# The last third of each layer's modulation on VectorE as products summed along rows, in place of TensorE

## The reference, cut to what matters

```
mod = (jax.nn.silu(cond) @ lw['w_ada'] + lw['b_ada'])[:, None, :]
shift1, scale1, gate1, shift2, scale2, gate2 = jnp.split(mod, 6, axis=-1)
h = rmsnorm(x, lw['norm_mix']) * (1 + scale1) + shift1
mix, new_ctx = token_mixers(h, lw, lam_init, ropes, ctx)
x = x + gate1 * (mix @ lw['w_out'])
h = rmsnorm(x, lw['norm_ffn']) * (1 + scale2) + shift2
x = x + gate2 * moe_ffn(h, lw)
```

## Time and profile before

| what | value |
|---|---|
| median of 3 runs | 1346.04 us (1345.32 to 1348.03) |
| the profiled execution's own time | 1347.21 us |
| its span, first to last instruction | 1345.4 us |
| TensorE busy | 1232.7 us (92%), mean granted clock 0.971 |
| VectorE busy | 273.3 us (20%) |
| ScalarE busy | 235.9 us (18%) |
| read from HBM | 493.60 MB |
| the chain that ended last | PE 69%, DMA 24%, DVE 2% |

### The profile page before, as it was taken

How to read it: one execution, slowest core, us unless ns; L and a number is a source line. 1 busy time by engine, 2 the same in 40 slices (tenths; PEclk the granted TensorE clock), 3 DMA queues, 4 the chain that set the end, 5 groups by cost and what they waited for, 6 DMA issues and landing times.

```text
span 1345.4 us, 22750 instructions
## 1 busy us (share of the span) xinstructions
PE 1232.7 (92%) x9612; PEld 841.1 (63%) x9612; DVE 273.3 (20%) x714; ACT 235.9 (18%) x521; POOL 2.8 (0%) x13
## 2 busy tenths in 40 slices
PE   6999999999998889888999999999999889888986
PEld 4566687667765565556565668866667565546554
DVE  1252342110011010101034424411011010101012
ACT  2363131110010101000134431311010101010102
POOL 0000000000000000000000000000000000000000
PEclk8999999999998899899999999999999999889999
DMA  9889849999999999999956663999999999999992
GB/s 385 323 318 343 349 190 403 372 422 420 421 420 422 422 422 422 422 421 422 410 203 260 246 242 151 416 373 420 421 418 420 422 422 420 420 422 423 421 420 93
DMA packets 80657, 496.58 MB, mean 369 GB/s; under 512 B 10576, under 2 KB 12880, under 8 KB 24784
## 3 DMA queue, kind: packets, MB, share of 16 engines
q1 hardware_dynamic: 76528, 493.63, 89.6%
q10 hardware_dynamic: 4064, 2.00, 0.5%
HBM read 493.60 MB, written 2.00 MB: 368 GB/s over the span
## 4 chain that ended last, share of the span: by engine, by line
PE 69%; DMA 24%; DVE 2%; issue 1%; SPq 1%; ACT 1%; DVEq 0%; ACTq 0%
DMA dn<-in_exp_w_down 20%; PE PS L2146 15%; PE PS L2180 13%; PE PS L2078 8%; PE PS L2085 7%; PE PS L1650 7%; PE PS L1982 4%; DMA gu<-in_exp_w_gate 3%; PE PS L1574 2%; PE PS L2044 2%; PE PS L1606 2%; DMA gu<-in_w_in 1%; PE PS L1773 1%; PE PS L1784 1%; PE PS L2122 1%
## 5 line engine op out<-in xcount | busy, mean ns | idle before, releaser
L2146 PE MATMUL PS<-gu,arena 128*32 128x256 f32 (+1 forms) x3072 | 318.5, 382 | 1.8 <-issue 1.8
L2146 PEld LDWEIGHTS PS<-gu,arena 128*32 128x32 f32 (+1 forms) x3072 | 186.6, 118 | 78.1 <-issue 19.7
L2180 PE MATMUL PS<-arena 128*64 128x512 f32 (+1 forms) x336 | 172.6, 662 | 61.4 <-DMA dn<-in_exp_w_down 59.8
L2180 PE MATMUL PS<-dn,arena 128*32 128x512 f32 (+1 forms) x688 | 180.4, 628 | 0.0
L2078 PE MATMUL PS<-arena 128*128 128x128 f32 x1408 | 176.3, 278 | 0.5 <-ACT arena L1024 0.5
L2078 PEld LDWEIGHTS PS<-arena 128*128 128x128 f32 x1408 | 164.1, 192 | 17.9 <-issue 16.7
L2085 PE MATMUL PS<-arena 128*128 128x256 f32 x704 | 160.2, 380 | 1.4 <-ACT arena L1006 1.4
L2146 PE MATMUL PS<-arena 128*64 128x256 f32 (+1 forms) x672 | 152.0, 379 | 0.0
L2085 PEld LDWEIGHTS PS<-arena 128*128 128x128 f32 x704 | 130.2, 190 | 20.5 <-ACT arena L1006 3.2
L1485 DVE TENSOR_TENSOR arena<-arena,PS 128x256 f32<-128x256 f32 x44 | 18.5, 421 | 563.4 <-ACT arena L1020 563.4
L1006 ACT ACTIVATE arena<-PS 128x512 f32<-128x512 f32 x88 | 52.5, 597 | 453.1 <-PE PS L2180 453.1
(11 more groups left out here) (257 smaller groups left out, 1022.9 us busy)
## 6 DMA issues: line engine op xcount, KB each, us to landing
gu<-in_exp_w_gate SPq DMA_DIRECT2D x106, 1024.0 KB, 16.0
gu<-in_exp_w_up SPq DMA_DIRECT2D x86, 1024.0 KB, 17.6
dn<-in_exp_w_down SPq DMA_DIRECT2D x86, 1024.0 KB, 17.6
arena<-in_exp_w_up SPq DMA_DIRECT2D x42, 1024.0 KB, 15.1
arena<-in_exp_w_down SPq DMA_DIRECT2D x42, 1024.0 KB, 17.1
gu<-in_w_ada SPq DMA_DIRECT2D x20, 2048.0 KB, 9.0
xh<-in_exp_w_gate SPq DMA_DIRECT2D x22, 1024.0 KB, 11.4
gu<-in_w_in SPq DMA_DIRECT2D x8, 2048.0 KB, 13.5
```

Of the source, the lines that this page charges most:

```text
L2146: ins = mmul(PS[w * h:w * h + w, 5, FF * half:FF * half + FF], xg[:, k, w * h:w * h + w], weights[half][:, k], start=(k == 0), stop=(k == ...
L2180: ins = mmul(PS[w * h:w * h + w, 7 - n, :], hidT[:, j * P + w * h:j * P + w * h + w], weights[:, j, 512 * n:512 * n + 512], start=(j == 0) ...
```

## The change

The third of the modulation that holds scale2 and gate2 leaves TensorE in both layers. The host turns its part of w_ada so that each partition holds, for one output element, the whole row of 1024 weights, and gives the conditioning as one row too. On the core, both conditioning vectors are broadcast over all partitions (1 MB, in a new tile cond_rows in the arena), ScalarE forms their Silu in place, and VectorE forms each output as a product of two 128x1024 operands that is summed along its row (accum_out): 8 chunks x 2 vectors x 2 groups, 32 instructions a layer. The weights come as four pieces "rows" of 2 MB through the same ring, in place of four modulation pieces. The products themselves go to a scratch tile. ROW_STEPS spreads the 32 steps over eleven places of VectorE's queue; the pieces 0 to 3 are freed by steps 8, 16, 24 and 32, the last of which stands behind the fourth update of x. ADA_AT has 8 pieces for layer 0 (from the third at P3) and 4 for layer 1, one of them in the norm; LOADED_EARLY is longer.

```
-ADA_AT = [{"P3": [4, 5], "P4": [6], "UQ": [7], "M": [8, 9], "P0a": [10], "P0b": [11], "P1a": [12, 13], "P1b": [14, 15]},
-          {"P3": [17], "P4": [18], "UQ": [19], "M": [20], "P0a": [21], "P0b": [22], "P1b": [23]}]
-ADA_NORM = {2: 16}
-ADA_BY = [4, 6]
+ADA_AT = [{"P3": [4, 5], "P4": [6], "UQ": [7], "P0a": [8, 9], "P0b": [10], "P1a": [11]},
+          {"P3": [13], "P4": [14], "UQ": [15]}]
+ADA_NORM = {2: 12}
+ADA_BY = [3, 4]
+ROW_STEPS = {"even3": 8, "even4": 4, "result4": 2, "masked": 5, "result5": 2, "mixed": 2, "keys": 2, "turned": 3,
+             "step1": 2, "step2": 1, "step3": 1}
 LOADED_EARLY = [(("w_in", 0, 2), ("chunks", 0, 2)), (("w_in", 0, 3), ("chunks", 0, 2)), (("mla", 0, 0), ("ada", 0, 6)),
-                (("w_in", 0, 0), ("ada", 0, 10)), (("w_in", 0, 1), ("ada", 1, 0))]
+                (("w_in", 0, 0), ("ada", 1, 0)), (("rows", 0, 0), ("ada", 1, 1)), (("w_in", 0, 1), ("ada", 1, 3)),
+                (("rows", 0, 1), ("ada", 1, 3)), (("w_out", 0, 1), ("rows", 0, 2)), (("w_out", 0, 0), ("rows", 0, 3)),
+                (("w_out", 1, 1), ("rows", 1, 2)), (("w_out", 1, 0), ("rows", 1, 3))]
...
-        out.append(("w_in", l, 0))
+        out += [("w_in", l, 0), ("rows", l, 0)]
         ada(l, "P0b", "P1a")
         out.append(("w_in", l, 1))
         ada(l, "P1b")
+        out += [("rows", l, q) for q in range(1, ROW_PIECES)]
         out += [("w_out", l, 1), ("w_out", l, 0)]
...
+                    if it == (("ada", 0, 4), ("mla", 1, 0))[l]:
+                        if l > 0:
+
+                            sp.wait_ge(S["down_done"], ROUNDS * l)
+                        sp.dma_start(cond_rows.rearrange("p g k -> p (g k)"), t["cond_rows"].partition_broadcast(P)
+                                     ).then_inc(S["cond_in"], 16)
...
                 for j in range(RING - 1):
-                    sp.wait_ge(S["weights_used"], ends[l] - RING + j + 1)
+                    wait_used(sp, last_in[l][j])
                     load_fixed(j, l)
...
                 exps(4)
+                act.wait_ge(S["cond_in"], 16 * (l + 1))
+                A(cond_rows, cond_rows, ACT.Silu).then_inc(S["cond_spread"], 1)
+
+                A(small[:, 501:502], col("eps"), ACT.Exp)
...
+            def ada_rows(l, at):
+
+                for _ in range(ROW_STEPS[at]):
...
+                    if i == 0:
+                        v.wait_ge(S["cond_spread"], l + 1)
+                    if j + g == 0:
+                        v.wait_ge(gu_loaded[item_slot[it]], loaded_at[it])
+                    ins = stt(products, gu[:, item_slot[it], j * D:j * D + D], 1.0, cond_rows[:, g], ALU.mult, ALU.mult,
+                              accum_out=mod[:, l, 4 + what, c, g:g + 1])
+                    if (j, g) == (ROW_CHUNKS - 1, G - 1):
+                        ins.then_inc(S["rows_used"], 1)
+                        v.wait_ge(S["rows_used"], ROWS_TOLD * l + 3 * what + q % 2 + 1)
+                        if c == NC_ - 1:
+                            tt(mod[:, l, 4 + what], mod[:, l, 4 + what], bc(b_ada[:, l, 4 + what], 2, G), ALU.add
+                               ).then_inc(S["rows_used"], 1)
+                    else:
+                        link(ins)
...
                 ada_lag(l, "P0a")
+                ada_rows(l, "even3")
                 latent_results(3)
                 even_half(4)
                 ada_lag(l, "P0b")
+                ada_rows(l, "even4")
                 negated_max(5)
...
                 ada_lag(l, "P1a")
+                ada_rows(l, "result4")
                 even_half(5)
...
                     if b > 0:
                         add_squares(STEPS[0][b - 1])
+                    if 0 < b < 4:
+                        ada_rows(l, f"step{b}")
```

## The result

The changed kernel takes 1371.24 us (median; 1369.84 to 1372.59) where the kernel before takes 1346.89 (1345.32 to 1348.03) in the same series: ratio 1.0174, 95% interval 1.016 to 1.0188, slower. That is +24.4 us; the forecast was +6.8. The profiled executions differ by 22.6 us (spans 1368.0 and 1345.4).

What follows compares the result with a forecast made beforehand. TensorE's chain was taken to bound each layer's first stage, weight bytes at 422 GB/s the expert stage. Layer 0: 0.7 + 5.0 - 4.5 = +1.2; layer 1: 3.1 + 5.0 - 2.5 = +5.6; 1346.04 + 6.8 = 1352.8 us, range 1337 to 1360.

Steps and rivals of the forecast that it cites:

- The product, 1.33 us: VectorE's 128x1024 product with row sum: 1.33 us a step, bounds 1.26 and 1.43, 42.6 us a layer.
- Rival C: Products with sum on VectorE run at half rate, each step 1.07 us more: 1400 us; chance 0.06.
- The stage up to the output projection: Before the expert stage: layer 0's gain shrinks from 8.4 to 0.6 us; layer 1's is lost, +0.5, +1.1 for the broadcast.
- Rows piece 1: Layer 0: this 2 MB weight piece lands at about 127.6 us and VectorE waits for it, 4 to 5 us.
- the maximum of unit 5: VectorE, layer 0: starts at 132.9 us, behind 4 steps, where it started at 127.40; +5.5.
- the broadcast: SyncE's 1 MB conditioning rows ahead of layer 1's latent weights: +1.1 us, bounded by 0 and 2.5; nothing in layer 0.
- The release, +0.7 and +3.1: Start of the expert weight stream: 186.7 us against 186.05 in layer 0, +3.1 us against 835.56 in layer 1.
- The one product that I had counted behind the updates: One VectorE step (1.33 + 0.03 us) behind the fourth update of x, counted in the release.
- The expert out of the hole, +5.0 less the gaps: Fixed expert 0's 2 MB load leaves the stream's hole: +5.0 us a layer, less 4.5 (layer 0) and 2.5 (layer 1).
- the gaps: Holes in the expert stream's first 60 us that a later stream fills: 4.5 us in layer 0, 2.5 in layer 1.
- VectorE against TensorE: First stage: VectorE's steps hold TensorE and eat the 8.4 us a layer taken from it.
- rival A: VectorE's steps fit its idle spans and don't hold TensorE, each layer keeps 8.4 us: 1334.6 us, faster; chance 0.22.

Runs made afterwards that it cites:

- e1: Changed kernel with VectorE's wait for the layer's six output stores moved from ahead of the first update of x to behind the last; 1362.96 us.
- e2: Changed kernel with SyncE waiting for the layer's six stores before it issues the shared weights, VectorE's wait left in place; 1361.92 us.
- e5: Kernel before, shared weights held until the retention output is turned, fixed expert 0 until the output weights are used, no new VectorE work; 1350.05 us.
- e14: Changed kernel with the edits of e1 and e12 together; 1359.46 us, +12.0 against the kernel before.
- e4: Kernel before with one wait changed: fixed expert 0 loaded only when the output weights are used up; 1349.15 us, +2.65.
- e6: Changed kernel with 36 matmuls of 2 columns with 128-column weights added at TensorE's start; 1383.71 us.
- e12: Changed kernel with 36 matmuls of 2 columns with 2-column weights added ahead of the first norm's sums in each layer; 1369.05 us.
- e7: Changed kernel with each product over 8 of its 1024 columns, loads, order and waits kept, third modulation vectors not the reference's; 1350.31 us.
- e10: Changed kernel with e1's edit, w_out piece 0 loaded ahead of rows piece 2, and products 17 to 32 behind the mix; 1363.94 us.
- e11: e10 with each product over 8 of 1024 columns, third modulation vectors not the reference's; 1338.02 us.

## Why the prediction was wrong

The direction was right, the size outside the range. Point by point:

**The product, 1.33 us: right enough.** 1224 ns, 1.27 from one to the next, near the lower end of my bounds. The read of the accumulator is recorded as 0.08 us and lies under the product's end. Rival C is dead, and by the same row so is the rule of the Trainium skill (Vector Engine (DVE) Microarchitecture Reference, section "Points that are easy to get wrong") for this case: by it the product would take twice as long and the kernel 1400 us; the trace doesn't agree, the form with a sum costs what the plain product costs.

**The stage up to the output projection: right in layer 1, 2.6 us short in layer 0.** Rows piece 1 was waited for until 127.12 (127.6 forecast), the maximum of unit 5 started at 132.20 (132.9); with the early start allowed for, both are about 1 us later than forecast. In layer 1, from its start, it was 93.6 where it was 92.7 before, and the output projection 116.9 where it was 115.5: +1.4, forecast +1.6 with the broadcast (TensorE waits 0.8 us for the latent weights, 1.1 forecast). In layer 0 the output projection is at 157.15, 2.0 us later than before when the early start is allowed for; forecast -0.6. The wait that the forecast had there is a little dearer than its length: TensorE idles 3.2 us for the scaled unit 5, and the granted clock is 0.62 behind it, so that the retention scores take 2.08 us for 1.09 and the second half of the projection 7.79 for 7.1. Busy time by stretch of after (clock, DMA share and GB/s last):

```profile
135.00:140.00 5.00, 2.45 (x12) 2.08 (x14) 3.99 (x8) 4.92 (x11) 0.00 (x0) 0.62 1.02 400
...
155.00:160.00 5.00, 2.85 (x7) 2.32 (x8) 4.31 (x9) 0.30 (x1) 0.00 (x0) 0.66 1.03 416
```

The second row is the start of the output projection. TensorE has idled 3.8 us for w_out, and the granted clock is 0.66 behind it: the first 24 records take 6.85 us where they took 5.42, in layer 1 7.03 for 5.24. The sum had nothing for this.

**The release, +0.7 and +3.1: mis-sized, and this is the step that failed.** Measured +8.4 in either layer (in layer 0 it would be +10.1 with an equal start), on top of what layer 1 inherited. I had let the updates of x start when TensorE had them ready, and counted one product before the sixth. I had asked what each new step is queued in front of, but not what moves with the slot that it frees. The shared weights stand behind rows piece 2 in the ring. That put their 3 MB from 152 to 170, 2 us ahead of ScalarE's three stores, and VectorE waits for those right before the first update. I had worked out where the loads for w_out and for expert 0 move, and not those of the shared weights between them. e1 and e2 show 8 to 9 us for it. e5 shows that it takes both halves: the late stores alone cost about 1.2, if anything. The one product that I had counted behind the updates was right: in e14 the last 80 records of the output projection start 4.3 us later than before (174.81 for 170.48) and the release is 5.5 later, 1.2 more. What is left of the miss, 4.8 us in layer 0, is the output projection. That e14's layer 1 came out at 3.4 for 3.1 is luck: the output projection starts 0.3 later there, not 1.6, and its first 24 records take 1.9 more.

**The expert out of the hole, +5.0 less the gaps: right.** e4 measures 2.65 for 3.0. In after the gaps give back 4.3 and 5.2 by the balance (4.5 and 2.5 forecast). Why the second is more than the gap that the rows of before showed stays open; it is a remainder, and holds what scatter there is.

**The branch, not in the sum at all: +4.4 by its row, 1.3 to 4.5 by the measured times.** Taking 36 matmuls out of TensorE's program moved the branch of layer 0's last round to a place where it costs 4.4 us. No row of before could size this, but its 0.5 us of "issue" at 665.58 was a hint that such a place is sensitive. By e6 and e12, an edit of this kernel's TensorE program can bring or take about 4 us here; that ought to stand in the range.

**VectorE against TensorE: right.** Between forecast and rival A lay 18.2 us for VectorE's time. The two pairs that differ in nothing else give 20.2 (after and e7) and 25.9 (e10 and e11).

So most of the miss of 17.6 us is two causes that the sum didn't have: with the stores and the branch taken away (e14) the change costs 12.0 us in place of 24.4. The other 5.2 us over the forecast are by the rows of e14's one profiled execution the output projection of layer 0, which is late and slow behind w_out; executions scatter by 2 to 3 us up to that place, so this part is less certain. The range of 1337 to 1360 would just have held e14, and not the stores and the branch on top.

## What to carry to other kernels

When a step moves that frees a buffer, follow the buffer: list what is loaded into it next, when that load will now go out, and which small transfers are in flight then, above all those that an engine waits for. A late load that nobody waits for can still cost, through a store that somebody does wait for; a wait for stores belongs as late as their buffers allow. And an engine with idle time has room for work only in front of waits that it would have had anyway; price the new work by taking its duration out, as e7 and e11 did, before tuning its places.

## What the hardware showed that was not expected

- Three stores of 256 KB in all take 2.2 to 2.3 us each in an idle stretch, and 7.7 to 9.2 us (5.6 to 9.8 in e5) when 3 MB of loads are issued within 2 us of them.
- Behind a branch TensorE stands still for 0.5 us in one program and for 4.4 in another with 36 matmuls fewer ahead of it, and 36 matmuls of padding move the cost to the other layer's branch.
- A product of two 128x1024 fp32 operands with its sum along the row takes 1224 ns, as the plain product does (1225), and 0.08 us for the accumulator, hidden.
- A matmul of 2 columns with 128-column fp32 weights is not free: 36 of them (72 records) took 15.5 us at the start of the program, 36 with 2-column weights 1.9.
- TensorE at half clock for 6 us in two norms cost nothing that could be measured, because the weight stream behind it was full.
